# Dividing each unit of expert weights between its two transfers by partitions instead of by half runs

## The reference, cut to what matters

```python
for e in range(N_EXPERTS):                       # 32
    hid = jax.nn.silu(t @ w_gate[e]) * (t @ w_up[e])     # w_gate, w_up: [1024, 512]
    y = y + combine[:, e:e + 1] * (hid @ w_down[e])      # w_down: [512, 1024]
```

## Time and profile before

| what | value |
|---|---|
| median of 3 runs | 2392.64 us (2389.26 to 2398.73) |
| the profiled execution's own time | 2391.92 us |
| its span in the profile | 2390.1 us |
| TensorE busy / its weight loads busy | 94% / 69% |
| VectorE / ScalarE busy | 50% / 36% |
| loop over the experts, first to last matmul on its weights | 523.8 to 994.0 us |

### The profile page before, as it was taken

The page is one execution under the profiler, slowest core; times in us unless marked ns, Lnnn a source line. Parts: engine busy times, 40 slices in busy tenths (PEclk is TensorE's granted clock), DMA queues, the critical chain, the costliest instruction groups (busy, mean ns, idle before and its releaser), DMA issues. The chain is left out here.

```text
span 2390.1 us, 31110 instructions
## 1 busy us (share of the span) xinstructions
PE 2236.7 (94%) x12298; PEld 1659.2 (69%) x12298; DVE 1192.3 (50%) x1997; ACT 852.6 (36%) x1445; POOL 21.3 (1%) x36
## 2 busy tenths in 40 slices
PE   6998899899999999799999999987999999999998
PEld 5686659665444444488888875444888888887887
DVE  1084224431111111367777741045777777787776
ACT  1111224321111111265554430034544555554454
POOL 1000000000000000000000010000000000000000
PEclk9999999999999999999999999998999999999999
DMA  9997576259999999945555462300444635635350
GB/s 338 355 354 275 204 278 249 106 218 418 422 422 422 422 422 422 384 146 208 162 177 190 167 198 73 100 3 1 153 167 155 212 107 211 229 127 191 108 210 36
DMA packets 237758, 540.27 MB, mean 226 GB/s; under 512 B 8910, under 2 KB 122136, under 8 KB 213064
## 3 DMA queue, kind: packets, MB, share of 16 engines
q1 hardware_dynamic: 234768, 531.66, 59.8%
q0 software_dynamic: 2192, 6.57, 1.0%
q10 hardware_dynamic: 680, 0.41, 0.1%
HBM read 537.55 MB, written 1.05 MB: 225 GB/s over the span
## 5 line engine op out<-in xcount | busy, mean ns | idle before, releaser
L980 PE MATMUL lo<-xs,wp 128*128 128x512 f32 x3904 | 690.5, 339 | 13.0 <-DVE wp L2006 9.8
L980 PEld LDWEIGHTS lo<-xs,wp 128*128 128x128 f32 x3904 | 597.7, 189 | 104.9 <-issue 14.1
L763 ACT ACTIVATE wp<-ring 128x1024 fp32r<-128x1024 f32 (+1 forms) x500 | 403.7, 832 | 318.6 <-PE hi L980 182.4
L2006 DVE TENSOR_TENSOR wp<-ring,wp 128x1024 fp32r<-128x1024 f32 (+1 forms) x500 | 459.3, 939 | 1.1 <-ACT wp L763 1.1
L980 PE MATMUL hi<-hs,wp 128*128 128x512 f32 x2016 | 369.4, 342 | 5.0 <-DVE hs L2222 3.2
L980 PE MATMUL lo<-ring,scratch 128*64 128x512 f32 x1536 | 336.2, 594 | 34.7 <-DMA ring<-in_moe_w_up_dram 23.2
L980 PEld LDWEIGHTS hi<-hs,wp 128*128 128x128 f32 x2016 | 311.4, 189 | 51.4 <-DVE hs L2222 3.6
L980 PEld LDWEIGHTS lo<-ring,scratch 128*64 128x64 f32 x1536 | 129.1, 137 | 230.8 <-issue 216.9
L980 PE MATMUL lo<-ht,ring 128*128 128x256 f32 (+1 forms) x704 | 169.9, 403 | 2.3 <-ACT ht L559 1.2
L980 PEld LDWEIGHTS lo<-ht,ring 128*128 128x128 f32 x704 | 134.4, 192 | 35.2 <-issue 15.2
L1968 DVE TENSOR_TENSOR scratch<-scratch,lo 128x512 f32<-128x512 f32 x16 | 17.4, 1088 | 195.8 <-PE lo L980 195.8
(11 more groups left out here) (360 smaller groups left out, 2071.8 us busy)
## 6 DMA issues: line engine op xcount, KB each, us to landing
ring<-in_mod_w_dram SPq DMA_DIRECT2D x72, 1024.0 KB, 10.4
ring<-in_moe_w_gate_dram SPq DMA_DIRECT2D x64, 1024.0 KB, 16.0
ring<-in_moe_w_up_dram SPq DMA_DIRECT2D x64, 1024.0 KB, 17.2
ring<-in_moe_w_down_dram SPq DMA_DIRECT2D x64, 1024.0 KB, 13.1
ring<-in_ffn_w_gate_dram SPq DMA_DIRECT2D x55, 1024.0 KB, 5.4
ring<-in_ffn_w_up_dram SPq DMA_DIRECT2D x55, 1024.0 KB, 8.4
ring<-in_ffn_w_down_dram SPq DMA_DIRECT2D x50, 1024.0 KB, 9.4
ring<-in_w_in_dram SPq DMA_DIRECT2D x20, 1024.0 KB, 9.1
```

The lines of the kernel that those rows point to most:

```text
L763: act.activation(wp[:, q % SLOTS, 0, k:k + w.shape[1], :], w, ACT.Copy).then_inc(piece_hi, 2 // len(parts))
L980: return pe.matmul(dst, lhsT, rhs, start=start, stop=stop, **kw)
L2006: tt(wp[:, q % SLOTS, 1, k:k + w.shape[1], :], w, wp[:, q % SLOTS, 0, k:k + w.shape[1], :].bitcast(F32), ALU.subtract).then_inc(piece_lo, ...
```

## The change

A new helper, `by_partitions`, replaces `split` for the experts' units alone. The first transfer of a unit now covers partitions 0 to 63 and the second 64 to 127, each with the whole 16 KB of a partition. The number of transfers, their size (1 MiB), their order, the slots, the semaphores and all waits stay the same. No other engine's program changes.

```diff
             with sp.Fori(0, EXPERTS // 2) as i:
-                for j, w, view, half in ((0, moe_w_gate, as_cols, 4), (2, moe_w_up, as_cols, 4), (4, moe_w_down, as_rows, 2)):
+                def by_partitions(v, s):
+                    return (v[0:P // 2], s[0:P // 2]), (v[P // 2:P], s[P // 2:P])
+
+                for j, w, view in ((0, moe_w_gate, as_cols), (2, moe_w_up, as_cols), (4, moe_w_down, as_rows)):
                     for e in range(2):
                         n = U_MOE + j + e
-                        load(n, lambda: split(view(n), expert_of(w, bass.ds(i * 2 + e, 1)), half), i)
+                        load(n, lambda: by_partitions(view(n), expert_of(w, bass.ds(i * 2 + e, 1))), i)
```

## The result

The changed kernel takes 2823.91 us (median of 4 runs, 2823.84 to 2832.04) against 2391.51 us for the kernel before; the ratio is 1.181 with an interval of 1.178 to 1.184. The forecast was 2821 us, in a range of 2600 to 2900 us. The profiled execution is the longest of the four, 2832.04 us with a span of 2830.2 us, so rows of it are to be set against the span of 2390.1 us of the kernel before: 440 us more. The other three runs are 8 us shorter, and no trace shows where.

The account below looks back on a forecast made before the run. The prediction took the DMA engines to bound the expert loop. At 214 GB/s its 188.7 MB take 882.0 us, ending the loop 429 us later: 2391.9 + 429 = 2821 us, range 2600 to 2900 us.

Parts of the forecast that it names:

- What bounds: Expert loop: full DMA engines set the 29.83 us period at 421.8 GB/s; a faster stream gives back at most 23.2 us.
- TensorE's own path: Expert loop: without its 1.85 us of wait, TensorE needs 27.98 us of each 29.83 us iteration.
- Longer runs: Expert loads: 16 KB packets need 612 ns, giving 428.1 GB/s and saving 6.5 us in all if nothing else changes.
- Half the partitions: Expert loads: writing 64 partitions at a time halves the rate to 214 GB/s; this half-rate case had chance 0.68.
- The bias loads: Sixteen loads covering 64 partitions, at 214 then 189 GB/s, DMA 0.78 and 0.82 busy; taken to suggest, not prove, a destination limit.
- The sum: Expert loop: 531.0 + 882.0 + 2.9 + 7.1 = 1423.0 us at its end, 429 us later than before.
- the lower bound of 2600 us: Low end of the whole-kernel range, reaching into partial engine drift, stated as 280 GB/s with 674 us of stream.
- TensorE's clock: Expert loop: a clock at 0.5 could stretch TensorE's path to 56 us, hidden under 58.8 except 7 us in the last group.
- Landing: Expert loop: expert units' transfers would land near 30 us after issue, as a sign in the profile after.
- Nothing but longer runs: Rival for the expert stream: no destination limit, 421.8 to 428.1 GB/s, 2385 to 2392 us; chance 0.13.
- Engines drift apart: Rival for the expert stream: engines in different halves win half the overlap, 321 GB/s, 2527 us; chance 0.12.
- The worst rival: Rival for the expert loop: 189 GB/s with TensorE's clock lowered, 2938 us, or 2945 with a cold last group; chance 0.07.

Follow-up runs that it names:

- experiment 5: Changed kernel with half of the experts' weights left out: a unit is one 1 MiB transfer to partitions 32 to 95; 2366.44 us.
- Experiment 1: Changed kernel with one 2 MiB transfer per unit to all 128 partitions, in runs of 16 KB; 2385.25 us, ratio 0.9974 to the kernel before.
- experiment 6: Changed kernel with half of the experts' weights left out: a unit is one 1 MiB transfer to partitions 0 to 63; 2403.42 us.
- experiment 3: Changed kernel with each unit's two transfers going to the even, then the odd partitions; 2380.49 us, again 2383.34 us over 9 runs.
- experiment 7: Changed kernel with four 512 KB transfers per unit, to partitions 0 to 31, 64 to 95, 32 to 63, 96 to 127 in turn; 2796.94 us.
- experiment 8: Changed kernel with lower halves issued by SyncE and upper halves by GpSimd from its own queue; 2732.49 us.
- experiment 4: Changed kernel with three transfers per unit: partitions 32 to 95, then 0 to 31 and 96 to 127; 2733.22 us.
- experiment 9: Changed kernel with only the down units divided by partitions, gate and up units by half runs as before; 2658.51 us.
- experiment 10: Changed kernel with only the second expert's unit of each pair divided by partitions, the first's by half runs; 2795.56 us.

## Why the prediction was right

*What bounds.* The DMA stream set the period before and sets it after, at a share of 1.0 in both. TensorE's 1.85 us of wait was indeed all that a faster stream could use: in experiment 5, whose stream has time to spare, the gate loads were issued 27.76 us apart, where the prediction had put TensorE's own path at 27.98.

*Longer runs.* The prediction gave 612 ns, 428.1 GB/s and 6.5 us for packets of 16 KB from rows for 2 and 8 KB. Experiment 1 measured 428 GB/s, and 5.5 us less than the kernel before (interval 3 to 9). Right, step and size.

*Half the partitions.* The rate was the choice, 214 GB/s. In the profile the last down units arrive at 1424.88 us, 892.9 us after the first gate loads of the steady stream at 532.03; less 2.9 us of landing, 188.7 MB in 890.0 us are 212.1 GB/s. The mechanism was the one forecast, a limit set by the half that is written: experiments 5 and 6 show it, 206 GB/s for the lower half alone. The number was partly luck. The bias loads left 189 to 428 GB/s open, and that their better window, 214 GB/s at a share of 0.78, equals half of 428.1 is chance as far as the rows show, since how fast GpSimd could issue (192 GB/s) had its part in it. They did point the right way, and more plainly than the prediction read them. Their pieces in the program are of 256 bytes, but the trace has these loads in packets of 4096 bytes, which took 270 ns in the mean, against the 159 ns of packets of that size to all 128 partitions. How much of that is the half and how much the small pieces isn't shown.

*The sum.* It was 1423.0 us for the loop's end; the profile has 1424.88 + 9.90 = 1434.8. The 11.8 us between are: 1.0 later start; 8.0 from 212.1 for 214 GB/s; 2.8 from the last group of matmuls, 9.90 us for 7.09. From the old end at 994.0 us that makes 440.8 of the 440.1 us by which the span grew, so nothing else moved, as forecast. The forecast meets the median within 3 us partly by luck, since the three unprofiled runs are 8 us shorter than the profiled one. A slip that changed nothing: by the prediction's own sum 280 GB/s gives 2613 us; the lower bound of 2600 us belongs to 285.

*TensorE's clock.* The granted clock fell to 0.72 to 0.80 in the loop, where TensorE is busy 34.7 of 60 us, and a group of 32 matmuls took 8.8 to 9.9 us for 7.1. As the rival supposed, this was hidden up to the last group. It is why the waits came to 371 us and not 462: of each iteration TensorE used 59.3 - 24.7 = 34.6 us, 6.6 more than its old path.

*Landing.* This sign of the profile was forecast wrongly, near 30 us for 41 to 42. A slot's round is now 59.3 us, of which TensorE uses it for 9: the down units issued at 782.92 us were used from 832.37 on, 49 us later. Nearly the whole round is queue and transfer, and doubling the old landing times missed that. The time of the kernel doesn't hang on it, because the stream stays full either way.

*The rivals.* "Nothing but longer runs" is what experiments 1 and 3 are, and it needs transfers that reach both halves. "Engines drift apart" would have shown as a higher rate: it is 4% more in experiment 7 and 13% in experiment 8, where the prediction allowed half of the overlap. The prediction's argument against it, that the slowest engine sets every landing, wasn't tested alone. The worst rival, 189 GB/s, didn't occur in any run that moved all weights.

Three expectations failed by their size. Experiments 4, 9 and 10 were summed as bytes over rate, each kind at its own rate, and were exceeded by 126, 121 and 186 us. Theory 3, that experiment 9's excess was a queue run dry, accounts at most for its idle share, some two thirds of that excess; experiment 10 has no idle engine and the larger excess.

## What to carry to other kernels

Divide a load so that every transfer reaches partitions on both sides of 64: by columns, by even and odd rows, or not at all; a transfer to the lower or the upper 64 has half the rate, and it slows full transfers that lie next to it in the queue. Don't price a mixed queue as bytes over rate: half of the units at half rate cost nearly as much as all of them. Longer runs are worth what a line through two packet sizes of the profile says, here 1.5% of a stream that was already full; even and odd partitions or one transfer of 2 MiB take 0.3% less than the kernel before and 16% less than the changed one, and can't be told apart.

## What was unexpected in the hardware

- 64 even partitions took the full 428 GB/s, the same as 128 in one transfer, and all 9 runs of it took 2377 to 2392 us.
- Packets of 8 KB to all partitions took 550 ns in the mean beside half transfers, for 314 among their like.
- Two queues with a half each, engines shared evenly (50.3% and 50.1%), reached 239 GB/s and not 428.
- After a gap in which the DMA engines stood idle, the first 16 packets of 16 KB took about twice as long as the ones behind them (1192 and 615 ns, experiment 5).
- With one half at a time, runs of 8 KB moved 216 GB/s and runs of 16 KB 212: the advantage of long packets, 1.5% at full width, is gone in these two traces.
